# Differential mixer: projection halves and early output units are given other blocks to run beside

## The chip, the cores and the metric

The kernel runs on one core of a Trainium2 chip. Its metric is the device time of one execution in microseconds (us). The engines are TensorE (PE, with its weight loads as PEld), VectorE (DVE), ScalarE (ACT), GpSimd (POOL) and SyncE (SP), which issues the transfers. Each runs its own instructions in the order of the program and waits for the others on semaphores.

## The reference

One layer of an encoder, 1024 tokens of width 1024, all in float32. What matters here is the mixer:

```python
xn = rms_norm(h, norm_mix[i])
proj = xn @ w_in[i]
qa, ka, va, qb, kb, vb = jnp.split(proj, SPLITS, axis=-1)
oa = sliding_window_sink_attention(qa, ka, va, sinks[i], bias_a)     # 8 heads, window 128
ob = differential_attention(qb, kb, vb, lam, ...)                    # 4 heads, 8 blocks of 128 queries
h = h + jnp.concatenate([oa, ob], axis=-1) @ w_out[i]

# differential_attention, for the 128 queries from qs, with all keys below qe = qs + 128:
sc = einsum('bqhmd,bkhmd->bhmqk', q[:, qs:qe], k[:, :qe]) * (HEAD_DIM ** -0.5)   # m = 0, 1
sc = where(allowed, sc + bias, NEG_INF)
pr = softmax(sc, axis=-1)
a = pr[:, :, 0] - lam * pr[:, :, 1]
outs.append(einsum('bhqk,bkhe->bqhe', a, v[:, :qe]))
```

A gated feed-forward part, a gate on a second input and a last norm follow.

## The kernel before

Every float32 product is made as three products of high and low parts (`SPLIT3`), so each operand is split by a copy on ScalarE (high part) and a subtraction on VectorE (low part).

**The differential mixer** is a loop over 32 blocks and a few more steps to drain it: block n is head n // 8 and query block n % 8, with n % 8 + 1 key tiles of 128. It is a pipeline over three iterations. In iteration n, PE runs `b_score(n)` (scores of both maps, into PSUM banks 1 to 4), then a filler, then the turning of earlier results (`y_turn`, the transposes on L1832), the transposes of block n - 1 (L1849) and the product of block n - 2 with V. Block n's scores wait until the exponentials of block n - 1 are done (`b_exp`), since there is one set of score banks. VectorE runs `b_diffs(n - 1)`, which starts with a RECIPROCAL (L1287), then the low part of the transposed block n - 2 (`a_t`), low parts of turned results, `b_logits(n)` (L1304 minima, L1306 bias and minimum, for both maps), then what belongs to fillers. ScalarE copies high parts and then runs `b_exps(n)` (L878). GpSimd normalises the results.

**Fillers.** Two kinds of work that belong to other stages are laid into this loop on PE:

- *Projection halves.* A unit is one 128-column tile of w_in times 512 tokens: 24 matmuls into bank 0, cut into two halves of 12. `b_fill(n)` says which half iteration n carries: 20 halves, two to a unit, in blocks 0 to 19. The last half of a unit is followed by its copy on ScalarE behind the block's exponentials (`unit_hi`) and its low part on VectorE (`unit_lo`, L1181 or L1179) ahead of the next reciprocal.
- *Early output units.* An output unit `c_unit(c)` is 6 matmuls, rows 0 and 1 of w_out times 128 tokens; VectorE adds its sum to `h` (`c_add`, L1319). There are 16: `c_units(n)` puts one in each of blocks 22 to 31 and two in each of iterations 32, 33 and 34. All up to unit 10 use bank 0, later ones banks 0 and 1 in turn (`c_bank`), and a unit waits until its bank's last sum is added. Unit 0 also waits for the reload of `mix_a` (transfers `mix_a_back`, `act_t<-mix_a`), and SP issues that once all projection units are done (`unit_done`, L508), as it overwrites their operand.

`WO_SPLITS` says in which iteration a row block of w_out is split; rows 0 and 1 wait for `unit_done` too, and unit 0 for them. After the last output unit (`c_done`, L522) SP reloads the second half of `mix_a`, for the rest of the output product. That stage, the feed-forward part and the gate follow.

On VectorE and ScalarE the order inside an iteration is that of the code:

```python
            if 2 <= n < NBS:
                b_logits(n)
            pending_w(n)
            part = b_fill(n)
            if part is not None and part % 2 == 1:
                unit_lo(FIRST_UNITS + part // 2)
            for c in c_units(n):
                c_add(c)
            for x in WO_SPLITS.get(n, ()):
                wo_low(x)
```

Of the kernel before, what the change touches and what calls it, by code (L numbers as in the profile page):

```python
# [23 lines left out]
KD = D // P  # L24
NT = SEQ // P
# [38 lines left out]
def build(nc, x, p, w_in, w_out, sinks, lambda_q, lambda_k, subln_gain, rel_bias, norm_mix, norm_ffn,  # L64
# [17 lines left out]
    first = ExitStack()  # L82
# [193 lines left out]
    S = type("S", (), sems)  # L276
# [20 lines left out]
    NUNIT = 2 * NTILE  # L297
# [3 lines left out]
    NA, NBS = 2 * NT, BH * NT  # L301

    HALVES = 2 * (NUNIT - FIRST_UNITS)

    def a_fill(n):
        return n if n < NA + 2 else None

    def b_fill(n):
        return NA + 2 + n if n < HALVES - NA - 2 else None


    def turned_with(n):
# [8 lines left out]
        return psf[:, at:at + P]  # L321

    C_ROWS = 2
    C_FROM = 22
    VIA_DRAM = 2 * NT

    def c_units(n):
        if n < C_FROM:
            return ()
        if n < NBS:  # L330
            return (n - C_FROM,)
        first = NBS - C_FROM + 2 * (n - NBS)
        return tuple(c for c in (first, first + 1) if c < 2 * NT)

    def c_bank(c):
        return c % 2 if c > NBS - C_FROM else 0


    O_ROWS = (4, 5, 6, 2, 3, 7)
    WO_ORDER = (0, 1) + O_ROWS  # L340

    WO_SPLITS = {20: (0,), 21: (1,), 25: (2,), 26: (3,), NBS + 1: (4,), NBS + 2: (5,), NBS + 3: (6,), NBS + 4: (7,)}

    def mix_dst(m, part):
        hh, i = m // NT, m % NT
# [451 lines left out]
    def _(act):  # L797
# [130 lines left out]
        for n in range(NBS + 5):  # L928
            if 2 <= n <= NBS + 1:
                act.wait_ge(S.b_turned, n - 1)  # L930
            for m in turned_with(n - 1):
                act.wait_ge(S.b_yturned, turned_with(n - 1)[-1] + 1)
                if 2 <= m < VIA_DRAM:
                    act.wait_ge(b_stored[m % 2], 16 * (m // 2))
                if m == VIA_DRAM:
                    act.wait_ge(S.unit_done, NUNIT)
                copy(mix_dst(m, 0), y_bank(n - 1, m), S.b_yhi)
            if 2 <= n <= NBS + 1:
                m = n - 2
                w = P * (m % NT + 1)  # L940
                act.wait_ge(S.b_turned, m + 1)
                if m >= 1:
                    act.wait_ge(S.b_pv, m)
                if m == 4:
                    act.wait_ge(S.a_stored, 16 * NA)
                copy(a_t[:, 0, 0:w], psf[:, 5 * HALF:5 * HALF + w], S.b_thi)
            if 3 <= n <= NBS + 2:
                m = n - 3
                act.wait_ge(S.b_pv, m + 1)
                if m >= 1:  # L950
                    act.wait_ge(S.b_sq, m)
                act.wait_ge(S.b_diff, m + 1)
                col = 4 * (m % 4)
                nc.scalar.activation(o_sb[:, :, :], ps[:, 7, 0:2 * P].rearrange("p (a q) -> p a q", a=2), ACT.Copy,  # L954
                                     scale=small[:, col:col + 1]).then_inc(S.b_part, 1)
            pending_w(n)
            for x in WO_SPLITS.get(n, ()):
                wo_hi(x)
            if 2 <= n < NBS:
                b_exps(n)  # L960
            part = b_fill(n)
            if part is not None and part % 2 == 1:
                unit_hi(FIRST_UNITS + part // 2)
            if 3 <= n <= NBS + 2:
                m = n - 3
                act.wait_ge(S.b_sum, m + 1)
                square(o_t[:, :], sq_out, stat[:, 16 + 3 * (m % 2):17 + 3 * (m % 2)], S.b_sq)
# [708 lines left out]
    def _(pe):  # L1676
# [38 lines left out]
        def unit(u, part=None):  # L1715
            j, half = u // 2, u % 2
            if part != 1:
                pe.wait_ge(S.w_lo, j + 1)
                if u == 0:
                    pe.wait_ge(S.xlo0, NT)  # L1720
                if u < FIRST_UNITS:
                    if u >= 2:
                        pe.wait_ge(S.unit_lo, u - 1)
                else:
                    pe.wait_ge(S.unit_lo, u)
            for k in range(KD) if part is None else range(KD // 2 * part, KD // 2 * (part + 1)):
                for n, (a, b) in enumerate(SPLIT3):
                    ins = mm(ps[:, unit_bank(u), :], w_sl[:, j % 2, a, k, :],
                             act_t[:, b, k, HALF * half:HALF * (half + 1)],
                             k == 0 and n == 0, k == KD - 1 and n == 2)  # L1730
            if part != 0:
                ins.then_inc(S.unit_done, 1)

        def c_unit(c):
            t, half = c // 2, c % 2
            if c == 0:
                pe.wait_ge(S.wo_lo, C_ROWS)
                pe.wait_ge(S.mix_c, 16 * 4 * C_ROWS)
                pe.wait_ge(S.unit_lo, NUNIT)
            elif c == NBS - C_FROM + 1:  # L1740
                pe.wait_ge(S.b_exp, 2 * NBS)
            else:
                pe.wait_ge(S.c_added, c - 1 if c_bank(c - 1) != c_bank(c) else c)
            for k in range(C_ROWS):
                for n, (a, b) in enumerate(SPLIT3):
                    ins = mm(ps[:, c_bank(c), :], act_t[:, a, k, t * P:(t + 1) * P],
                             wo(k, b)[:, HALF * half:HALF * (half + 1)], k == 0 and n == 0, k == C_ROWS - 1 and n == 2)
            ins.then_inc(S.c_done, 1)
# [85 lines left out]
        for n in range(NBS + 2):  # L1834
            if 2 <= n < NBS:
                b_score(n)
            if b_fill(n) is not None:
                unit(FIRST_UNITS + b_fill(n) // 2, b_fill(n) % 2)
            for c in c_units(n):
                c_unit(c)  # L1840
            if 2 <= n <= NBS + 1:
                pe.wait_ge(S.b_tlo, n - 1)
            y_turn(n)
            if 1 <= n <= NBS:
                m = n - 1
                nk = m % NT + 1
                pe.wait_ge(S.b_diff, m + 1)
                for k in range(nk):
                    ins = nc.tensor.transpose(psf[:, 5 * HALF + k * P:5 * HALF + (k + 1) * P],  # L1849
                                              e_t[:, m % 2, 0, k * P:(k + 1) * P], ident[:, :])  # L1850
                ins.then_inc(S.b_turned, 1)
            if 2 <= n <= NBS + 1:
                m = n - 2
                hb, nk = m // NT, m % NT + 1
                if m == 0:
                    pe.wait_ge(S.a_olo, NA)
                pe.wait_ge(S.b_tlo, m + 1)
                if m >= 1:
                    pe.wait_ge(S.b_part, m)
                for k in range(nk):  # L1860
                    mm(ps[:, 7, 0:2 * P], a_t[:, 0, k * P:(k + 1) * P], v_b[:, k, hb, :], k == 0, False)
                    ins = mm(ps[:, 7, 0:P], a_t[:, 1, k * P:(k + 1) * P], v_b[:, k, hb, 0:P], False, k == nk - 1)
                ins.then_inc(S.b_pv, 1)

        def oproj(i, rows):
            t = O_TILE[i]
# [260 lines left out]
```

## Time and profile before

| | us |
|---|---|
| median of 3 runs (1274.5 to 1275.2) | 1275.17 |
| the profiled execution | 1275.12 |
| its span, first to last instruction | 1273.3 |
| PE busy | 1213.6 (95%) |
| PEld busy | 993.5 (78%) |
| DVE busy | 875.3 (69%) |
| ACT busy | 519.1 (41%) |
| POOL busy | 321.3 (25%) |
| granted TensorE clock, mean | 0.994 |

Busy is the time in which an engine had an instruction in work. The 32 blocks of the differential mixer run from about 205 to 407 us of the span. A row of the trace in order of time tells the start, the length, the engine, the line, the operation, what it writes and reads and in what shape, how many like it stand together, and in brackets how long the engine was idle before and who ended that wait. Line numbers are those of the kernel before. Matmul rows of different shapes at one line are merged where they follow each other, so the shape is that of the first.

### The profile page before, as it was taken

How to read it: one execution, taken by the hardware profiler on the slowest of the kernel's cores; microseconds unless marked ns; L12 is line 12 of the kernel's file. 1: busy time of each engine (PE TensorE's matmuls, PEld its weight loads, DVE VectorE, ACT ScalarE, POOL GpSimd, SP SyncE). 2: the span in 40 equal slices, each digit the busy share in tenths (PEclk: the TensorE clock that was granted, in tenths of full speed). 3: DMA queues.
4: the chain of work that ended last, by engine and by line, in shares of the span. 5: the costliest groups of instructions: out<-in, count | busy, mean ns of one | idle time of the engine just before them, and what ended most of it. 6: DMA issues, size and time to landing. Idle time of an engine off the chain costs nothing.

```text
span 1273.3 us, 16978 instructions
## 1 busy us (share of the span) xinstructions
PE 1213.6 (95%) x6103; PEld 993.5 (78%) x6103; DVE 875.3 (69%) x1466; ACT 519.1 (41%) x1042; POOL 321.3 (25%) x335
## 2 busy tenths in 40 slices
PE   4999999999789899999999999999999999999997
PEld 3997787788567777888888888888887768888885
DVE  3432786876787477877787777877769997864442
ACT  3322665565564224433333333333344434633321
POOL 0000000354455122232322323313217870000000
PEclk9999999999899999999999999999999999999999
DMA  7364132112831511333322333323497534520101
GB/s 205 73 98 95 42 92 68 46 42 71 210 130 40 159 50 55 104 110 97 121 87 83 124 100 108 98 85 108 149 357 250 166 102 137 186 75 25 42 34 50
DMA packets 128669, 136.08 MB, mean 107 GB/s; under 512 B 15570, under 2 KB 93130, under 8 KB 128522
## 3 DMA queue, kind: packets, MB, share of 16 engines
q1 hardware_dynamic: 128586, 135.00, 35.3%
q8 instruction: 49, 0.80, 0.3%
q14 instruction: 34, 0.28, 0.1%
HBM read 96.77 MB, written 37.22 MB: 105 GB/s over the span
## 4 chain that ended last, share of the span: by engine, by line
PE 56%; DVE 8%; issue 3%; DMA 1%; ACT 0%; SPq 0%; POOL 0%; POOLq 0%; DVEq 0%; ACTq 0%
PE ps L1678 54%; DVE wbuf L1179 4%; DVE more L1179 1%; DVE h L1604 1%; DMA raw<-u_ops 1%; PE ps L1688 1%; DMA act_t<-mix_a 1%; DVE xs L1463 0%; PE ps L1899 0%; DVE h L1458 0%; DVE conv L1402 0%; SPq L479 0%; POOL stat L678 0%; ACT xs L802 0%; DVE act_t L1179 0%
## 5 line engine op out<-in xcount | busy, mean ns | idle before, releaser
L1678 PE MATMUL ps<-act_t,wbuf 128*128 128x512 f32 x1200 | 288.8, 396 | 2.9 <-DVE wbuf L1179 2.9
L1678 PEld LDWEIGHTS ps<-act_t,wbuf 128*128 128x128 f32 x1200 | 225.7, 188 | 57.4 <-issue 3.3
L1678 PE MATMUL ps<-wbuf 128*128 128x512 f32 x912 | 217.5, 392 | 2.6 <-DVE wbuf L1179 2.5
L1678 PEld LDWEIGHTS ps<-wbuf 128*128 128x128 f32 x912 | 170.0, 188 | 42.0 <-DVE wbuf L1179 5.3
L1678 PE MATMUL ps<-act_t,wq 128*128 128x512 f32 x624 | 155.7, 402 | 3.6 <-DVE wq L1181 2.8
L1678 PEld LDWEIGHTS ps<-act_t,wq 128*128 128x128 f32 x624 | 114.6, 189 | 33.5 <-issue 7.3
L1179 DVE TENSOR_TENSOR wbuf<-raw,wbuf 128x512 fp32r<-128x512 f32 (+1 forms) x107 | 104.8, 980 | 13.4 <-ACT wbuf L799 13.1
L678 POOL TENSOR_TENSOR stat<-stat 128x1 f32<-128x1 f32 x32 | 17.6, 549 | 347.6 <-DVE stat L1188 347.6
L799 ACT ACTIVATE wbuf<-raw 128x512 fp32r<-128x512 f32 (+1 forms) x107 | 69.2, 648 | 88.2 <-PE ps L1678 70.4
L1678 PE MATMUL ps<-hx,wbuf 128*128 128x512 f32 x408 | 96.2, 391 | 0.0
L1678 PEld LDWEIGHTS ps<-hx,wbuf 128*128 128x128 f32 x408 | 76.5, 188 | 16.6
L1678 PE MATMUL ps<-wbuf,act_t 128*128 128x512 f32 x288 | 72.7, 407 | 3.2 <-DMA act_t<-mix_a 3.2
L878 ACT ACTIVATE e_t<-ps,small 128x128 f32<-128x128 f32 (+7 forms) x64 | 47.3, 740 | 62.3 <-DVE small L1306 61.2
L799 ACT ACTIVATE wbuf<-xs 128x512 fp32r<-128x512 f32 x66 | 39.8, 624 | 76.6 <-DVE xs L1402 54.2
L1678 PEld LDWEIGHTS ps<-wbuf,act_t 128*128 128x128 f32 x288 | 54.0, 192 | 16.1 <-issue 3.6
L1678 PE MATMUL ps<-wq,act_t 128*128 128x384 f32 (+1 forms) x384 | 59.5, 315 | 0.3 <-DVE act_t L1179 0.3
L1678 PEld LDWEIGHTS ps<-wq,act_t 128*128 128x128 f32 x384 | 57.8, 193 | 0.7 <-DVE act_t L1179 0.7
L1678 PE MATMUL ps<-act_t,more 128*128 128x512 f32 x240 | 58.2, 395 | 0.0
L694 POOL TENSOR_TENSOR o_t<-o_sb 128x128 f32<-128x128 f32 x32 | 14.7, 458 | 170.8 <-ACT o_sb L954 166.8
L705 POOL TENSOR_TENSOR wbuf_f<-wbuf_f 128x512 f32<-128x512 f32 x33 | 52.0, 1576 | 19.0 <-DVE wbuf_f L1542 16.0
L1179 DVE TENSOR_TENSOR a_t<-ps,a_t 128x512 fp32r<-128x512 f32 (+4 forms) x64 | 44.6, 715 | 17.7 <-ACT a_t L799 17.5
L1678 PEld LDWEIGHTS ps<-act_t,more 128*128 128x128 f32 x240 | 45.2, 188 | 10.6
(197 smaller groups left out, 2043.9 us busy)
## 6 DMA issues: line engine op xcount, KB each, us to landing
u_ops<-wbuf_f SPq DMA_DIRECT2D x77, 256.0 KB, 2.2
raw<-u_ops SPq DMA_DIRECT2D x77, 256.0 KB, 2.7
raw<-in_w_ffn_in SPq DMA_DIRECT2D x33, 512.0 KB, 3.9
g_ffn<-in_w_ffn_in SPq DMA_DIRECT2D x11, 512.0 KB, 4.1
act_f<-in_w_ffn_out SPq DMA_DIRECT2D x21, 256.0 KB, 3.9
w_raw<-in_w_in SPq DMA_DIRECT2D x10, 512.0 KB, 4.5
wbuf_f<-in_w_ffn_out SPq DMA_DIRECT2D x18, 256.0 KB, 6.6
x_in<-in_x SPq DMA_DIRECT2D x8, 512.0 KB, 3.6
```

The lines of the kernel that those rows point to most:

```text
L678: nc.gpsimd.tensor_tensor(dst, src, stat[:, 63:64], ALU.pow).then_inc(done, 1)
L694: nc.gpsimd.tensor_tensor(o, o_sb[:, 0, :], o_sb[:, 1, :], ALU.add).then_inc(S.b_sum, 1)
L705: nc.gpsimd.tensor_tensor(dst, a, b, ALU.subtract).then_inc(done, 1)
L799: nc.scalar.activation(dst, src, ACT.Copy, scale=scale).then_inc(done, 1)
L878: nc.scalar.activation(e_t[:, pr, m, 0:w], psf[:, at:at + w], ACT.Exp, scale=-1.0, bias=small[:, o + 2 + m:o + 3 + m], accum_out=small[:, ...
L1179: ins = nc.vector.tensor_tensor(dst, src, hi.bitcast(F32), ALU.subtract)
L1604: nc.vector.tensor_tensor(h[:, t, HALF_X[n]], ps[:, banks(r)[i % 4], :], h[:, t, HALF_X[n]], ALU.add).then_inc(S.h_fin, 1)
L1678: return nc.tensor.matmul(dst, lhs, rhs, start=start, stop=stop)
L1688: ins = nc.tensor.transpose(psf[:, bank * HALF + k * P:bank * HALF + (k + 1) * P], src[:, k * P:(k + 1) * P], ident[:, :])
```

## The change

The 20 projection halves go to blocks 0 to 6, 8 to 14 and 16 to 21: blocks 7 and 15, which have 8 key tiles, lose theirs, and 20 and 21 get one. The 16 output units start in block 25 instead of 22: one in block 25, two in each of 26, 27 and 28, one in 29, none in 30 and 31, then two, three and three. In iterations with more than one, PE runs the first where it stood, ahead of the transposes, and the others behind the product with V; VectorE's order stays as it is. All up to unit 8 use bank 0. The splits of w_out rows move by one or two blocks. The last unit takes its operand's tiles 4 to 7 first, and ScalarE's first write into that operand waits for that half alone (`vproj`) instead of for all units.

```diff
+    B_FILL = dict(zip((0, 1, 2, 3, 4, 5, 6, 8, 9, 10, 11, 12, 13, 14, 16, 17, 18, 19, 20, 21), range(NA + 2, HALVES)))
+
     def b_fill(n):
-        return NA + 2 + n if n < HALVES - NA - 2 else None
+        return B_FILL.get(n)
...
-    C_FROM = 22
...
+    C_FIRST = {25: 0, 26: 1, 27: 3, 28: 5, 29: 7, 30: 8, NBS: 8, NBS + 1: 10, NBS + 2: 13, NBS + 3: 16}
+
     def c_units(n):
-        if n < C_FROM:
-            return ()
-        if n < NBS:
-            return (n - C_FROM,)
-        first = NBS - C_FROM + 2 * (n - NBS)
-        return tuple(c for c in (first, first + 1) if c < 2 * NT)
+        return tuple(range(C_FIRST[n], C_FIRST[n + 1])) if n in C_FIRST and n + 1 in C_FIRST else ()

     def c_bank(c):
-        return c % 2 if c > NBS - C_FROM else 0
+        return c % 2 if c > C_FIRST[NBS] else 0
...
-    WO_SPLITS = {20: (0,), 21: (1,), 25: (2,), 26: (3,), NBS + 1: (4,), NBS + 2: (5,), NBS + 3: (6,), NBS + 4: (7,)}
+    WO_SPLITS = {22: (0,), 23: (1,), 26: (2,), 27: (3,), NBS + 1: (4,), NBS + 2: (5,), NBS + 3: (6,), NBS + 4: (7,)}
...
                 if m == VIA_DRAM:
-                    act.wait_ge(S.unit_done, NUNIT)
+                    act.wait_ge(S.vproj, NT + 1)
...
-            for k in range(KD) if part is None else range(KD // 2 * part, KD // 2 * (part + 1)):
+
+            order_k = (4, 5, 6, 7, 0, 1, 2, 3) if u == NUNIT - 1 else range(KD)
+            ks = order_k if part is None else order_k[KD // 2 * part:KD // 2 * (part + 1)]
+            for k in ks:
...
             if part != 0:
                 ins.then_inc(S.unit_done, 1)
+            elif u == NUNIT - 1:
+                ins.then_inc(S.vproj, 1)
...
-            elif c == NBS - C_FROM + 1:
+            elif c == C_FIRST[NBS] + 1:
                 pe.wait_ge(S.b_exp, 2 * NBS)
...
-            for c in c_units(n):
+            for c in c_units(n)[:1]:
                 c_unit(c)
...
                 ins.then_inc(S.b_pv, 1)
+            for c in c_units(n)[1:]:
+                c_unit(c)
```

## Rows read from the trace of the kernel before

**Rows 1.** In order of time, PE alone: scores of blocks 12 and 20 and those after.

```profile
276.96 1.25 PE L1678 MATMUL ps<-wq 64*128 64x512 f32 x12
...
282.33 1.31 PE L1678 MATMUL ps<-wq 64*128 64x512 f32 x12
...
323.29 1.25 PE L1678 MATMUL ps<-wq 64*128 64x512 f32 x12
...
328.67 1.31 PE L1678 MATMUL ps<-wq 64*128 64x512 f32 x12 [1.15 <-ACT e_t L878]
```

**Rows 2.** The same view, blocks 22 to 24: scores, units 0 and 1, transposes of 23.

```profile
334.22 1.49 PE L1678 MATMUL ps<-wq 64*128 64x512 f32 x12 [0.66 <-ACT e_t L878]
339.23 2.90 PE L1678 MATMUL ps<-act_t 128*128 128x512 f32 x6 [3.52 <-issue]
...
346.49 1.65 PE L1678 MATMUL ps<-act_t 128*128 128x512 f32 x6
...
354.23 1.06 PE L1849 MATMUL ps<-ident,e_t 128*128 128x128 f32 x8 [0.79 <-DVE a_t L1179]
```

**Rows 3.** In order of time, SP's queue: the two reloads of `mix_a`.

```profile
326.04 6.64 SPq L479 DMA_DIRECT2D act_t<-mix_a  x8
...
407.04 5.58 SPq L479 DMA_DIRECT2D act_t<-mix_a  x8
```

**Rows 4.** In order of time, VectorE: the reciprocals of blocks 21 to 23, 29 to 31.

```profile
334.19 0.17 DVE L1287 RECIPROCAL small<-small 128x2 f32<-128x2 f32 x1
...
342.84 0.15 DVE L1287 RECIPROCAL small<-small 128x2 f32<-128x2 f32 x1
...
351.19 0.17 DVE L1287 RECIPROCAL small<-small 128x2 f32<-128x2 f32 x1 [0.72 <-ACT e_t L878]
...
380.86 0.17 DVE L1287 RECIPROCAL small<-small 128x2 f32<-128x2 f32 x1 [0.52 <-ACT e_t L878]
...
387.01 0.17 DVE L1287 RECIPROCAL small<-small 128x2 f32<-128x2 f32 x1 [0.62 <-ACT e_t L878]
...
393.80 0.17 DVE L1287 RECIPROCAL small<-small 128x2 f32<-128x2 f32 x1 [0.73 <-ACT e_t L878]
```

**Rows 5.** In order of time, ScalarE and VectorE: the end of block 15.

```profile
300.65 1.12 ACT L878 ACTIVATE e_t<-ps,small 128x1024 f32<-128x1024 f32 x1
...
302.38 0.69 DVE L1181 SCALAR_TENSOR_TENSOR wq<-ps,wq 128x512 fp32r<-128x512 f32 x1 [1.76 <-ACT wq L799]
302.99 0.15 DVE L1287 RECIPROCAL small<-small 128x2 f32<-128x2 f32 x1
```

**Rows 6.** By stage: stretch, PE, PEld, DVE, ACT, POOL busy (count), PEclk, DMA share, GB/s.

```profile
324.50:335.70 11.20, 5.93 (x51) 4.87 (x49) 10.92 (x26) 8.21 (x20) 5.84 (x10) 1.00 0.88 173
335.70:337.20 1.50, 0.01 (x2) 0.00 (x0) 1.50 (x3) 0.00 (x0) 1.32 (x3) 1.00 1.29 244
337.30:343.90 6.60, 4.67 (x16) 4.02 (x17) 3.41 (x10) 2.73 (x7) 2.31 (x6) 0.50 1.11 316
```

**Rows 7.** In order of time, PE: product with V in iteration 31, transposes, units 14 and 15.

```profile
391.27 1.57 PE L1678 MATMUL ps<-v_b,a_t 128*128 128x256 f32 x12
...
396.84 1.06 PE L1849 MATMUL ps<-ident,e_t 128*128 128x128 f32 x8 [0.68 <-DVE a_t L1179]
...
404.07 2.94 PE L1678 MATMUL ps<-act_t 128*128 128x512 f32 x12
```

**Rows 8.** In order of time, VectorE and PE: w_out low part, end of block 28.

```profile
365.13 1.22 DVE L1179 TENSOR_TENSOR wbuf<-raw,wbuf 128x1024 fp32r<-128x1024 f32 x1
...
373.85 0.49 DVE L1306 CUSTOM_DVE_ANT_0 ps<-ps,bias_b,small 128x256 f32<-128x256 f32 x1
...
374.01 0.89 PE L1678 MATMUL ps<-v_b,a_t 128*128 128x256 f32 x6
...
374.28 0.69 DVE L1319 TENSOR_TENSOR h<-ps,h 128x512 f32<-128x512 f32 x1
...
375.35 0.17 DVE L1287 RECIPROCAL small<-small 128x2 f32<-128x2 f32 x1 [0.38 <-ACT e_t L878]
```

More of the change, by code:

```diff
@@ L1729, in unit @@
                              act_t[:, b, k, HALF * half:HALF * (half + 1)],
-                             k == 0 and n == 0, k == KD - 1 and n == 2)
+                             k == order_k[0] and n == 0, k == order_k[-1] and n == 2)
             if part != 0:
                 ins.then_inc(S.unit_done, 1)
+            elif u == NUNIT - 1:
+                ins.then_inc(S.vproj, 1)
         def c_unit(c):
```

## Prediction, made before the changed kernel was run

> **What bounds the kernel now.** I first read the row of 40 slices on the page: TensorE is nearly always busy, so I looked for the stretch that the change touches, the 32 blocks of the differential mixer, block n having n mod 8 + 1 key tiles. Everything outside it is taken as unchanged. There the list of PE's waits and the order of its work in time tell two regimes apart. Where a block with few or middling keys carries a projection half, PE has no idle time: no row of block 12 shows any [rows 1]. From block 20 on it waits ahead of most scores. Its longest wait, 3.52 us and put down to "issue", is that of early output unit 0 in block 22: PE ends the scores at 335.7 and starts the unit at 339.23 [rows 2]. What it waits for is the reload of `mix_a`, whose eight transfers SP issues over 326.04 to 332.7 [rows 3], because it waits for the last projection half, at the end of block 19.
>
> In blocks with many keys VectorE sets the pace, not PE. A block's clock is best read at its RECIPROCAL (L1287): the vector engine then runs, in order, the difference, two low parts, two maxima and two bias additions without a gap and waits only for the second exponential. From one reciprocal to the next it is 6.15 us with 7 key tiles (380.86 to 387.01) and 6.79 with 8 (387.01 to 393.80); blocks 22 and 23 instead took 8.65 and 8.35 (334.19, 342.84, 351.19) [rows 4].
>
> **Part 1: halves taken out of blocks 7 and 15.** A unit's last half also costs VectorE: in block 15 the exponentials end at 301.77 (300.65 + 1.12), but the vector engine first waits for ScalarE's copy of the unit and makes the low part (302.38, 0.69), so the reciprocal starts at 302.99, 1.1 us later than the 0.12 after the exponentials of an undelayed block [rows 5]. Taking the half away gives 1.1 us back at each of blocks 7 and 15. But the units that end at odd blocks 9 to 15 now end at even ones 8 to 14, and their copies delay those: in block 14 VectorE loses 1.1 it did not lose before. Walking the blocks with these durations, with PE-bound ones (unchanged) between, 0.7 us of the first gain is used up by block 13, and 0.5 us is left from block 16 on. Blocks 16 to 19 have the same halves as before, so block 19 ends 0.5 us earlier.
>
> **Part 2: halves in blocks 20 and 21.** Block 12, with a half, takes PE from score to score 276.96 to 282.33, 5.37 us; block 20, without one, 323.29 to 328.67, 5.38 [rows 1]. The half fills time in which PE waited, so it costs nothing. The second half's low part delays the reciprocal of block 21 by 1.1: 334.19 - 0.5 + 1.1 = 334.8. The splits of w_out rows 0 and 1 go two blocks later with it, into the exponentials' time of blocks 22 and 23, and cost about 0.
>
> **Part 3: the stall at unit 0.** SP now sees the last unit done 6.5 us later, at about 332.5, so the reload is issued until 339.1 and lands, with the same 6.5 us behind the last issue as before (332.7 to 339.2), at about 345.6. Queued behind it on SP are the residual rows, the reload of `mix_b` and the w_out rows; they move with it, and their users (block 26 on, and the output product) have over 10 us to spare. Unit 0 stands in block 25, where PE arrives at about 354: the wait is gone. Blocks 22 and 23 run at the undisturbed pace: 334.8 + 6.15 = 340.95, + 6.79 = 347.7, against 351.19. **Shift here: -3.5 us.** The new wait of ScalarE (`vproj` instead of `unit_done`, block 21) is over before it gets there, since the first half of the last unit runs in block 20.
>
> **Part 4: blocks 22 to 24 now hold nothing but their own work.** The granted clock was 1.00 over 324.5 to 335.7, with PE at work 5.93 of 11.2 us, and still in the first 1.5 us of the wait for unit 0; from 337.3 to 343.9 it was 0.50, 1.2 GHz [rows 6]. At the low clock six matmuls took 2.90 us for 1.65 [rows 2]. After the change PE is emptier still around block 24: block 23's product with V ends at about 346.8 (340.95 + 5.83, as 391.27 + 1.57 stands behind 387.01 [rows 4, 7]), six small score matmuls run at 347.8 for 0.55, and the next transposes wait for VectorE until 350.7 (347.7 + 3.04, as 354.23 behind 351.19 [rows 2, 4]). I take one fall of the clock there, felt by 2.6 us of transposes and products that the path goes through. Halving it over part of them costs between 1.1 and 1.7; I take 1.4. The bounds are 0 and the 3.3 that half of 337.3 to 343.9 would be. **Shift after block 25: -2.1.**
>
> **Part 5: pairs of output units in blocks 26, 27 and 28.** PE runs the second unit of a block behind the product with V, and it must wait until the first one's sum is added, as both use bank 0. On VectorE `c_add` of both stands behind the block's bias additions and ahead of the next reciprocal. So the vector engine adds the first sum, waits while PE makes the second, adds that, and only then goes on. In block 28 the first add starts at 374.28; the second unit could start at 374.97 (PE has just finished the product with V, 374.01 + 0.89), takes 1.65, its add starts at 376.75 and the reciprocal at 377.35 instead of 375.35: 2.0 us [rows 8, 2]. In block 27 it is the same chain, 2.0, plus the low part of a w_out row that now stands there, 1.22 [rows 8], together 3.2. In block 26 there was such a row before: 2.5. Taken off: that row leaves block 25, worth 0.4. Sum 2.0 + 3.2 + 2.5 - 0.4 = **7.3 us**, all on VectorE's chain, with the next blocks' score, exponential and transposes behind it. The bounds: 0, if the second unit were done before the bias additions end, and 3 x (0.69 + 1.65 + 0.69) + 1.2 = 10.3 if none of it lay under the exponentials; I take 7.3, as it is worked out from the rows of these same blocks.
>
> What this buys is nothing: in blocks 30 and 31 a unit lay in PE's idle time and its add under the exponential, so 6.15 and 6.79 were reached with it [rows 4]. **Shift at the end of block 31: -2.1 + 7.3 = +5.2.**
>
> **Part 6: the end.** Before, six units stood behind block 31; now eight. In the old frame: unit 8 lies in the gap ahead of the transposes at 396.84, 9 and 10 take the place of 12 and 13, five follow the product with V instead of two: 3 x 1.47 = 4.4 us (404.07 + 2.94 for two) [rows 7]. The add of unit 9 stands ahead of block 31's low part and delays the two y transposes by 1.0, and unit 15 waits 0.3 for its bank. +5.7. SP issues the reload of the second half of `mix_a` only after the last unit, at 407.04 [rows 3], and what follows is of fixed length. So the whole shift stays.
>
> Sum: -3.5 + 1.4 + 7.3 + 5.7 = **+10.9 us**. The profiled execution took 1275.12 (span 1273.3, 1.8 around it), as good as the median of 1275.17; 1275.12 + 10.9 = **1286.0 us**, 0.85% slower.
>
> **Rivals.**
> (a) *The clock falls only once PE does no work at all.* Speaking for it: of the two falls each came in a wait of over 3 us. Against: it had fallen 1.6 us into the wait that began at 335.7 [rows 6]. Part 4 is then 0: 1284.6. The Trainium skill, "TensorE: Matmul & The Clock Gate", section "HAM oscillation — how this bites in real kernels", has this rule, a clock that falls after an idle stretch. By it too the emptied block 24, with its six small matmuls, would keep the clock. The trace of before agrees only loosely, by the instant of the fall just given.
> (b) *The clock falls more often.* PE also gets waits of some 2 us in blocks 15 and 28 and behind block 31, near or above the longest at which it held before block 22. Each fall costs up to 1.7 where PE sets the pace, as behind block 31, and less elsewhere: 1287.5 to 1291.
> (c) *Not slower.* One mechanism, in blocks 26 to 28: the second unit is ready by the time VectorE asks for it, so that a pair costs nothing. It decides at the point where the product with V ends 2.4 us (a unit and an add) before the bias additions do. The whole 7.3 goes, 1278.7, and with no fall of the clock 1277.3, within 0.2% of before. Against it: in block 28 the product ended at 374.90 and the additions at 374.34 [rows 8], and bank 0 has to be emptied in between.
> (d) *The change doesn't do what it says*: unit 0 meets its reload still under way. By Part 3 there are 8 us between, though SP's transfers share the DMA engines with the residual rows. A late one costs what it is late, 1287 to 1290.
>
> **How the numbers follow.** The forecast 0.53, (a) 0.12, (b) 0.16, (c) 0.12, (d) 0.02, and 0.05 for a gain that I don't see. (c) lies half within 0.2% and half above it. That gives faster by over 0.2% 0.05, within it 0.06, slower 0.89; 0.2% (2.5 us) is about what a measurement of this kernel can tell from no change. The range reaches from the upper end of (c), 1278.5, to most of (b), 1290, with the upper bounds of Part 4 (1287.9) and Part 5 (1289.0) inside; it leaves out some 0.15.
>
> **What would show it.** The reciprocal of block 23 at about 347.7, and no PE wait on "issue" there; a granted clock of 0.5 near 350; a VectorE wait of about 1.7 on PE ahead of an `h` addition (L1319) in each of blocks 26, 27 and 28, and their reciprocals 2 us and more behind the exponentials; block 31's about 5 us later than 393.80; the second reload issued near 418. It is wrong above all if those VectorE waits are missing, or if the tail behind block 31 isn't longer by more than the two units.

## The result, and the profile after

The changed kernel takes 1295.84 us (median of 4 runs, 1294.18 to 1296.66) against 1274.94 for the kernel before (4 runs, 1274.5 to 1275.2): ratio 1.0160, 95% interval 1.0145 to 1.0174. It is slower, as forecast, but by 20.9 us and not by 10.9, and outside the range. The profiled execution took 1295.2 with a span of 1293.4, so 20.1 us above the span of before. Later runs of the changed kernel without any alteration gave 1290.27 (1288.46 to 1296.99, 4 runs), 14.4 above the kernel before beside them (ratio 1.0127). So it is not a narrow number, and I come back to that (e6); the forecast is too low by either.

The page of the changed kernel, its row of TensorE's busy time and of its granted clock in 40 slices of 32 us:

```profile
span 1293.4 us, 16978 instructions
...
PE   4999999899787899999999999999999999999997
...
PEclk9999999998888899899999999999999999999999
```

The five 8s, slices ten to fourteen, are 291 to 453 us: the second half of the differential mixer and the stretch behind it. By stage, the mixer, first in the changed kernel, then in the one before (columns as in [rows 6]):

```profile
203.00:425.00 222.00, 194.00 (x1158) 158.42 (x1157) 155.03 (x383) 117.10 (x322) 88.03 (x160) 0.92 0.27 79
```

```profile
203.00:407.00 204.00, 182.68 (x1159) 148.78 (x1158) 153.44 (x382) 117.32 (x322) 87.62 (x158) 0.98 0.30 86
```

VectorE and ScalarE are busy nearly as long as before; PE does the same matmuls and needs 11.3 us longer, at a mean clock of 0.92 instead of 0.98. So far more matmuls ran slowed than I had reckoned with. What of it lay on the path, busy time doesn't say.

VectorE's reciprocals of blocks 21 to 23 and 29 to 31 in the changed kernel, in order of time, for [rows 4]:

```profile
336.58 0.15 DVE L1285 RECIPROCAL small<-small 128x2 f32<-128x2 f32 x1
...
342.82 0.17 DVE L1285 RECIPROCAL small<-small 128x2 f32<-128x2 f32 x1 [0.18 <-ACT e_t L876]
...
350.01 0.17 DVE L1285 RECIPROCAL small<-small 128x2 f32<-128x2 f32 x1 [0.19 <-ACT e_t L876]
...
391.48 0.17 DVE L1285 RECIPROCAL small<-small 128x2 f32<-128x2 f32 x1 [0.51 <-ACT e_t L876]
...
397.63 0.17 DVE L1285 RECIPROCAL small<-small 128x2 f32<-128x2 f32 x1 [1.17 <-ACT e_t L876]
...
404.54 0.17 DVE L1285 RECIPROCAL small<-small 128x2 f32<-128x2 f32 x1 [1.27 <-ACT e_t L876]
```

The two kernels stand 0.15 us apart already at block 6, ahead of the change; all shifts below are taken from there. Block 21 is 2.2 us later than before (expected +0.6), block 23 1.3 earlier (expected 3.5), block 31 10.6 later (expected 5.2). The last output unit's addition comes 18.0 us later (expected 10.9), the stretch behind it, with the second reload and the matmuls that follow, is 1.2 longer, and the rest of the kernel 0.8.

The change has its own wait of VectorE. VectorE's work in block 27 of the changed kernel, in order of time:

```profile
372.62 0.49 DVE L1304 CUSTOM_DVE_ANT_0 ps<-ps,bias_b,small 128x256 f32<-128x256 f32 x1
...
373.03 0.69 DVE L1317 TENSOR_TENSOR h<-ps,h 128x512 f32<-128x512 f32 x1
375.54 0.69 DVE L1317 TENSOR_TENSOR h<-ps,h 128x512 f32<-128x512 f32 x1 [1.82 <-PE ps L1676]
376.15 1.40 DVE L1177 TENSOR_TENSOR wbuf<-raw,wbuf 128x1024 fp32r<-128x1024 f32 x1
377.47 0.15 DVE L1285 RECIPROCAL small<-small 128x2 f32<-128x2 f32 x1
```

This is the chain that Part 5 worked out: first sum, 1.82 us of waiting for PE's second unit, second sum, low part of a w_out row, and only then the reciprocal.

And the clock. Stretches of the changed kernel in which it was granted 0.50, 1.2 GHz, all of them before 600 us:

```profile
299.50:306.20 6.70, 5.83 (x23) 4.97 (x23) 4.77 (x13) 4.72 (x13) 3.25 (x5) 0.50 0.68 245
340.50:347.10 6.60, 5.18 (x24) 3.93 (x23) 5.96 (x11) 4.55 (x10) 3.12 (x5) 0.50 1.17 265
354.10:360.80 6.70, 6.70 (x29) 5.67 (x28) 2.74 (x8) 2.67 (x10) 2.29 (x5) 0.50 1.06 389
381.40:388.10 6.70, 6.12 (x21) 4.39 (x22) 3.19 (x8) 2.19 (x7) 2.28 (x5) 0.50 0.01 4
395.10:398.30 3.20, 3.20 (x18) 3.08 (x16) 1.93 (x8) 2.65 (x7) 0.36 (x3) 0.50 0.00 0
408.70:412.00 3.30, 3.30 (x16) 3.20 (x15) 0.00 (x0) 0.74 (x3) 1.82 (x4) 0.50 0.00 0
436.00:442.70 6.70, 5.53 (x13) 4.39 (x14) 1.24 (x2) 1.06 (x1) 0.00 (x0) 0.50 0.51 178
518.00:524.60 6.60, 5.88 (x15) 4.64 (x16) 3.07 (x5) 0.63 (x1) 0.00 (x0) 0.50 0.02 5
```

Six falls lie in the mixer, where before had one (the wait for unit 0) and I had forecast one. The seventh stands at the end of the wait for the second reload; before had one there too, at 419, but 3.4 us long. The eighth has no counterpart in before.

### The profile page after: what moved, and what is told of

Same layout as the page of the kernel before. It is cut to its first block, busy times and chain, and to the rows that moved or that the text cites. A ratio compares the mean times of both kernels' runs of the same rounds, so it can differ in the third digit from the quotient of the medians.

```text
span 1293.4 us, 16978 instructions
## 1 busy us (share of the span) xinstructions
PE 1227.9 (95%) x6103; PEld 1006.2 (78%) x6103; DVE 877.5 (68%) x1466; ACT 518.2 (40%) x1042; POOL 319.8 (25%) x335
## 4 chain that ended last, share of the span: by engine, by line
PE 53%; DVE 9%; issue 3%; DMA 1%; SPq 1%; ACT 0%; POOL 0%; POOLq 0%; DVEq 0%; ACTq 0%
PE ps L1676 52%; DVE wbuf L1177 5%; DVE more L1177 1%; DVE h L1602 1%; PE ps L1686 1%; DMA raw<-u_ops 1%; DMA act_t<-mix_a 1%; DVE xs L1461 0%; PE ps L1904 0%; DVE h L1456 0%; DVE conv L1400 0%; SPq L477 0%; POOL stat L676 0%; DVE act_t L1177 0%; ACT xs L800 0%
## 5 line engine op out<-in xcount | busy, mean ns | idle before, releaser
L1177 DVE TENSOR_TENSOR wbuf<-raw,wbuf 128x512 fp32r<-128x512 f32 (+1 forms) x107 | 106.5, 997 | 12.4 <-ACT wbuf L797 12.1
L1676 PEld LDWEIGHTS ps<-act_t,more 128*128 128x128 f32 x240 | 45.2, 188 | 10.6
```

The costliest lines, as they stand in the source:

```text
L1177: ins = nc.vector.tensor_tensor(dst, src, hi.bitcast(F32), ALU.subtract)
L1676: return nc.tensor.matmul(dst, lhs, rhs, start=start, stop=stop)
```

## The experiments

My theory after the result: Parts 1 to 3, 5 and 6 hold, and what is missing is the clock, which falls wherever the change leaves PE half empty. The rival: a pair of units, or the shifted halves, cost more than worked out, and the clock only shows it. In the table, "block 23" and "block 31" are the shifts of these blocks' reciprocals against before, and "last unit" that of VectorE's addition of output unit 15. The shifts of a kernel are read from one profile of it; its times are of all its runs.

| kernel | median us (range; runs) | ratio, 95% interval | block 23 | block 31 | last unit |
|---|---|---|---|---|---|
| changed | 1295.8 (1294.2–1296.7; 4) | 1.0160 (1.0145–1.0174) | −1.3 | +10.6 | +18.0 |
| e6, the same again | 1290.3 (1288.5–1297.0; 4) | 1.0127 (1.0099–1.0155) | −1.5 | +9.5 | +15.3 |
| e1, waits filled | 1287.7 (1284.9–1289.5; 4) | 1.0095 (1.0072–1.0118) | −3.4 | +5.6 | +11.4 |
| e2, late addition | 1284.9 (1284.2–1285.8; 4) | 1.0076 (1.0056–1.0095) | −1.9 | +4.1 | +9.9 |
| e3, single units | 1281.0 (1278.9–1285.6; 5) | 1.0051 (1.0028–1.0073) | −1.5 | −1.2 | +4.6 |
| e4, old halves | 1290.8 (1287.4–1291.4; 4) | 1.0112 (1.0086–1.0139) | −4.0 | +6.9 | +14.3 |
| e5, old halves, singles | 1281.2 (1279.3–1283.6; 4) | 1.0053 (1.0036–1.0069) | −4.0 | −3.6 | +2.2 |
| e7, before filled | 1275.1 (1272.1–1279.0; 10) | 0.9996 (0.9984–1.0008) | −2.2 | −2.2 | −2.2 |
| e8, from 23, filled | 1274.4 (1272.8–1275.8; 10) | 0.9989 (0.9980–0.9999) | −4.0 | −4.0 | −2.6 |
| e9, e8 without filler in the reload wait | 1275.3 (1270.5–1278.8; 11) | 0.9991 (0.9979–1.0002) | −4.1 | −4.1 | −2.7 |
| e10, from 23 alone | 1275.0 (1271.2–1279.1; 12) | 0.9990 (0.9977–1.0004) | −2.9 | −2.9 | −1.6 |

Beside them, on their chips, the kernel before took 1275.7 (e1 to e4), 1275.9 (e5 to e8) and 1276.3 (e9, e10); the ratios are against that.

**e1_filled: the clock alone.** The changed kernel, with matmuls whose result nobody reads laid into PE's waits. They stand where PE waits anyway, and write a bank that is free there.

```diff
+        WARM = {15: (12, 4), 22: (10, 4), 23: (8, 4), 24: (14, 0), 30: (10, 4), 31: (6, 4), 32: (14, 0)}
...
+            for _ in range(WARM[n][i]):
+                mm(ps[:, 2 if n == NBS else 0, 0:2 * P], v_b[:, 0, 0, 0:P], v_b[:, 1, 0, :], True, True)
```

> The changed kernel with matmuls whose results nobody reads (128 x 256, into a bank that is free at that time) laid into the blocks that the change emptied: 16 in block 15, 14 in 22, 12 in 23, 14 in 24, 14 in 30, 10 in 31, 14 behind unit 8. They fill waits of PE and nothing else is changed. Theory A (the low clock is the missing part: the walk without any fall gives +9.5 us at the last output unit, the trace shows +18.0): the falls near 299, 340, 354, 395 and 408 us go, the one near 381 stays, some 7 us come back, about 1289. Theory B (the missing part lies in VectorE's chain and in waits; the low clock falls mostly on work that was not on the path): no gain, 1295 or more. Up to 3 us of loss under both if the added matmuls delay the transposes.

Measured: 1287.73, 8 us under the changed kernel's first median and 2.5 under its second (e6), near theory A's 1289. By stage, the mixer and the first stretches at which the clock had fallen, and the one at which it still fell:

```profile
203.00:418.00 215.00, 194.18 (x1252) 158.93 (x1251) 154.59 (x382) 116.96 (x322) 88.25 (x160) 0.99 0.28 82
299.50:306.20 6.70, 5.48 (x37) 4.63 (x37) 4.61 (x13) 4.87 (x14) 3.27 (x5) 1.00 0.66 248
340.50:347.10 6.60, 5.57 (x44) 4.80 (x44) 6.28 (x13) 4.69 (x11) 3.12 (x5) 1.00 1.13 300
354.10:360.80 6.70, 6.37 (x42) 5.13 (x41) 5.58 (x19) 4.66 (x15) 3.18 (x7) 1.00 1.02 408
377.50:380.80 3.30, 3.30 (x12) 2.16 (x12) 0.54 (x1) 1.28 (x5) 2.28 (x5) 0.50 0.00 0
```

With 94 matmuls more, the mixer is shorter. The reciprocals of blocks 23 and 31 in this kernel, in order of time:

```profile
347.71 0.17 DVE L1285 RECIPROCAL small<-small 128x2 f32<-128x2 f32 x1 [0.19 <-ACT e_t L876]
...
399.33 0.17 DVE L1285 RECIPROCAL small<-small 128x2 f32<-128x2 f32 x1 [1.27 <-ACT e_t L876]
```

347.71 is the 347.7 of Part 3. 399.33 is 1.7 us above what Parts 1 to 5 give without a fall of the clock (393.80 − 3.5 + 7.3 = 397.6); the fall left at 377.5 is 1.0 of it (below). The clock accounts for 6.7 us at the last unit (18.0 − 11.4, rounded from 18.01 − 11.35) and this 1.0, 7.7 in all. The rival had the whole gap in the pairs or halves, and that is refuted. The 7.7 belongs to the changed kernel's first profile: the second one (e6) stands 3.9 us above e1 at the last unit, so that the clock cost it 4.9 (3.9 and the same 1.0).

**e2_late_add: the pairs' wait.** In blocks 26 to 28 VectorE adds the second unit behind the next block's differences, one iteration later, instead of ahead of its reciprocal.

```diff
             if 2 <= n <= NBS:
                 b_diffs(n - 1)
+            if n - 1 < NBS:
+                for c in c_units(n - 1)[1:]:
+                    c_add(c)
...
-            for c in c_units(n):
+            for c in c_units(n)[:1] if n < NBS else c_units(n):
                 c_add(c)
```

> The changed kernel, but VectorE adds the second sum of blocks 26, 27 and 28 behind the next block's differences instead of ahead of its reciprocal, so it no longer stands still for PE. Theory A (VectorE's wait of 1.8 us for the second unit plus its add stands on the chain, three times; 3.4 in block 28): reciprocals of 26, 27 and 28 come 2.4 us or more earlier after their exponentials, and 5 to 8 us go, 1288 to 1291. Theory B (PE then waits for that add ahead of the next block's first unit and the transposes behind it are as late as before): within 2 us of the changed kernel, 1294 to 1296.

Measured: 1284.94. VectorE in blocks 26 and 27, in order of time:

```profile
366.52 0.69 DVE L1317 TENSOR_TENSOR h<-ps,h 128x512 f32<-128x512 f32 x1
367.12 1.22 DVE L1177 TENSOR_TENSOR wbuf<-raw,wbuf 128x1024 fp32r<-128x1024 f32 x1
368.25 0.16 DVE L1285 RECIPROCAL small<-small 128x2 f32<-128x2 f32 x1
...
369.24 0.68 DVE L1317 TENSOR_TENSOR h<-ps,h 128x512 f32<-128x512 f32 x1
...
373.83 0.16 DVE L1285 RECIPROCAL small<-small 128x2 f32<-128x2 f32 x1
```

The second addition at 369.24 waits for nothing, and from reciprocal to reciprocal it is 5.58 us. In e1 the same two stand at 364.96 and 372.63, 7.67 apart. So the wait was real, and it was the order on VectorE that made it. The additions themselves stay, and block 31 is at +4.1. The total is 10.9 us under the changed kernel's first median, more than theory A's 5 to 8, and 5.3 under its second. Not all of it is the wait: the clock was low at 304.1 and from 351.9 to 362.1 in this profile and nowhere else before 430, so the falls near 340, 381, 395 and 408 are missing too. How much of this the late addition did, and how much is chance (see e6), one profile can't tell.

**e3_singles: no pairs.** The changed kernel with its halves, but one output unit in each of blocks 24 to 31.

```diff
-    C_FIRST = {25: 0, 26: 1, 27: 3, 28: 5, 29: 7, 30: 8, NBS: 8, NBS + 1: 10, ...}
+    C_FIRST = {24: 0, 25: 1, 26: 2, 27: 3, 28: 4, 29: 5, 30: 6, 31: 7, NBS: 8, NBS + 1: 10, ...}
```

> The changed kernel with its 8 early output units one to a block in blocks 24 to 31 instead of in pairs in 26 to 28; the eight behind block 31 as they are. Theory A (pairs cost some 8.4 us on VectorE's chain without the clock, and the emptied blocks 24, 30 and 31 lower the clock): both go, 1281 to 1284. Theory B (pairs are cheap, the tail is what costs): 1292 or more. In either case it stays above the kernel before, for the tail's 5.7 us less the 3.5 of the stall: 1277 or more.

Measured: 1281.03, as theory A had it, and 6.7 under e1 although the clock still falls at 298.2 and 339.1. From block 25 to 31 it becomes 1.1 later against before. The units in blocks 24 and 25, and in 30 and 31, cost nothing, and they keep PE busy: no fall lies between 346 and 424.

**e4_old_halves: the other half of the change.** The halves stay in blocks 0 to 19, the units are placed as in the changed kernel.

```diff
-    B_FILL = dict(zip((0, 1, 2, 3, 4, 5, 6, 8, 9, 10, 11, 12, 13, 14, 16, 17, 18, 19, 20, 21), range(NA + 2, HALVES)))
+    B_FILL = dict(zip(range(20), range(NA + 2, HALVES)))
```

> The changed kernel with the projection halves where they were, in blocks 0 to 19, and the new place of the output units. Theory A (moving the halves gives 0.5 us less than 1.1 at block 21, and costs the fall of the clock near 299, some 2 us; but without them blocks 20 to 24 are all empty and the clock falls there once more): within 2.5 us of the changed kernel, 1293 to 1298. Theory B (the halves beside 1024 keys cost time of their own, as the change's name has it): 3 us or more slower than the changed kernel.

Measured: 1290.76, like e6, so theory B is out; the 1293 of theory A was not reached either, by either kernel. With block 15's half back there is no fall at 299. With no halves in 20 and 21 the falls come at 325.6 and 349.5 instead, and then at 370.0, 390.4, 404.1, 3.4 us each. So one thinned stretch is exchanged for another.

**e5_old_singles: old halves and single units.** Both edits above together; what is left of the change is that the units begin in block 24.

> Both moves undone but the number of units: projection halves in blocks 0 to 19, early output units one to a block in blocks 24 to 31, the eight behind block 31 as in the changed kernel. Against the run with single units and the new halves it shows the halves alone. Theory A (the new halves cost the fall of the clock behind block 15 and the unit's low part at block 21, a few us): 1277 to 1279. Theory B (the halves' move is neutral, as the walk ahead of the prediction had it, -0.5 then +1.1): 1280 to 1282. By the sum of parts: -4.0 for the stall, +5.8 for the longer end, so 1.8 above the kernel before.

Measured: 1281.22, which is theory B's number, the same as e3, whose halves are the changed kernel's. In the profiles theory A has something for it: block 23 is 2.4 us earlier than in e3, and the last unit too. That does not show in the total, of which both have a spread of over 4 us. At the last unit the profile stands at +2.2, near the 1.8 of the sum of parts; the profile has 1.4 more behind it and 0.6 ahead of block 6. Against e4 it is 9.5 less: that is what the pairs, with the falls around them, cost.

**e6_after_again: the changed kernel once more,** no edit.

> The changed kernel once more, unaltered, beside the others of this set, since the kernel before spread from 1272 to 1278 us in the last one. Every theory: 1293 to 1298, 19 to 22 us above the kernel before of the same set.

Measured: 1290.02, 1290.52, 1288.46 and 1296.99; three of the four lie under what every theory had. The profile shows falls at 298.4, 339.4, 353.0, 380.3 and 390.6, of 6.8, 6.8, 3.4, 3.4 and 6.8 us: five and not six in the mixer, two of them half as long. The same instructions meet another number of falls in another execution. Behind block 31, for example, PE waited 2.72 us in the changed kernel and the clock fell at 408.7; in e6 it waited 2.92 and the clock stayed at 1.00. TensorE there in order of time, first in the changed kernel, then in e6:

```profile
407.59 1.06 PE L1852 MATMUL ps<-ident,e_t 128*128 128x128 f32 x8 [2.72 <-DVE act_t L1177]
```

```profile
405.89 1.06 PE L1852 MATMUL ps<-ident,e_t 128*128 128x128 f32 x8 [2.92 <-DVE act_t L1177]
```

Between the two profiles the falls make 2.7 us at the last unit, of 5.2 us in all. That the clock makes the whole 5.6 us between the medians, or the 8.5 between single executions, is not shown: one run of the changed kernel took 1296.66 us at a mean clock of 0.987, one of e6 1290.52 at 0.988.

**e7_before_filled: is the clock worth anything before the change?** The kernel before with unread matmuls in blocks 20 to 22, and 12 more ahead of the wait for the second reload.

```diff
+        WARM = {20: (10, 6), 21: (12, 3), 22: (24, 0)}
...
+                            for _ in range(12):
+                                mm(ps[:, 4, 0:P], ident[:, :], ident[:, :], True, True)
                         pe.wait_ge(S.mix_23, 16 * 8)
```

> The kernel before with matmuls whose results nobody reads laid into PE's waits: 16 in block 20, 15 in 21, 24 in 22 ahead of unit 0, and 12 small ones ahead of the wait for the second reload of mix_a. All waits stay as long as they were. Theory A (a low clock costs what the slowed matmuls lose on the path: 2.5 us behind the stall at unit 0, up to 1.7 behind the second wait): 2 to 4 us faster than the kernel before. Theory B (what the clock costs is hidden behind VectorE): no difference.

Measured: 1275.1, ratio 0.9996, no difference. That is theory B's number, but not its reason. The fall at 337 is gone and block 23 is 2.2 us earlier, where 2.5 was expected, and this lasts until the last unit (−2.2). Then it is given back: in the profile the reload, from the last unit's addition on, took 13.4 us (404.49 to 417.88) instead of 11.7. The clock fell behind it for 3.4 us, as in before, and once more at 499.7, where before it did not:

```profile
417.88 14.29 PE L1678 MATMUL ps<-wbuf,act_t 128*128 128x512 f32 x53 [2.18 <-DMA act_t<-mix_a]
```

```profile
417.70:421.10 3.40, 3.22 (x8) 2.56 (x9) 1.12 (x1) 1.06 (x1) 0.00 (x0) 0.51 0.12 47
499.70:503.10 3.40, 3.40 (x11) 2.62 (x10) 1.29 (x2) 0.47 (x1) 0.00 (x0) 0.50 0.00 0
```

**e8_from23_filled, e9_from23_blocks, e10_from23: the good part alone.** The stall at unit 0 can be removed without pairs and without moving a half: units from block 23 on, one each, and seven behind block 31. e8 adds both kinds of filler, e9 those in blocks 20 to 22 only, e10 none.

```diff
-    C_FROM = 22
+    C_FROM = 23
...
-        return tuple(c for c in (first, first + 1) if c < 2 * NT)
+        if n == NBS + 2:
+            return tuple(range(first, 2 * NT))
+        return tuple(c for c in (first, first + 1) if c < 2 * NT) if n < NBS + 2 else ()
...
-        return c % 2 if c > NBS - C_FROM else 0
+        return (c - NBS + C_FROM) % 2 if c > NBS - C_FROM else 0
```

> The kernel before with the early output units one block later, 23 to 31 (nine, and seven behind them), halves as they were, and unread matmuls in the waits of blocks 20 to 22 and ahead of the second reload. Unit 0 should then meet a reload that has landed. Theory A (the stall's 4.0 us go, one more unit at the end costs 1.5, the clock does not fall, 2 to 4): 1269 to 1272. Theory B (the end grows by more than the one unit, as the adds stand ahead of the last low part): 1273 or more.

> Output units from block 23 on and unread matmuls in blocks 20 to 22, as in the last set's fastest, but nothing laid into the wait for the second reload of mix_a. There, both kernels with matmuls in that wait had a reload of 13.4 and 13.6 us, against 11.7 to 11.9 in the others. Theory A (the matmuls in the wait slow the transfers down): the reload takes 11.7 to 11.9 again, the clock falls behind the wait, and the two cancel: 1273 to 1275. Theory B (the longer reload has another cause): 13 us or more here too, 1275 to 1277.

> The kernel before with its early output units in blocks 23 to 31 and seven behind them, and nothing else changed or added. Theory A (the stall of block 22 goes, -4.0; one more unit behind block 31 +1.4; the clock falls once near 337 while blocks 20 to 22 are empty, +1 or less as it meets work hidden behind VectorE): 1273 to 1275.5. Theory B (the fall of the clock takes back what the stall gave): 1275.5 or more.

Measured: 1274.42, 1275.30 and 1274.95, ratios 0.9989, 0.9991 and 0.9990. Only e8's interval ends under 1, at 0.9999; these are a tenth of a per cent, if anything, and no clear winner. e8 came out as theory B had it, e9 between its two theories, e10 as theory A. The table says why: the stall gives 4.0 us with the filler (2.9 without, as the clock still falls at 337.0), the seventh unit behind block 31 takes 1.4 of it, and the fall of the clock at 497 to 499 or the longer reload takes more. The reload took 13.6 us in e8, 12.4 in e9 and 12.0 in e10. That the fillers in the wait lengthen it is the likely reading of e7 and e8, but it rests on one profile each, and the cause stays open.

## Why the prediction was wrong, step by step

**Part 1** (+1.1 back at blocks 7 and 15, 0.5 left) held: blocks 7 and 15 each gain 1.1, block 16 stands 0.9 earlier in both profiles of the changed kernel, where the walk had 0.5, and block 17 0.5 earlier in e1. That last figure is of a kernel with unread matmuls in block 15; no run has the new halves there with neither them nor a fall. **But it missed what block 15 became.** With no half and eight key tiles PE is nearly empty there, and the clock fell at 299.5. TensorE in that place in the changed kernel, in order of time:

```profile
294.46 1.66 PE L1676 MATMUL ps<-wq 64*128 64x512 f32 x12
298.18 0.30 PE L1835 MATMUL ps<-ident,bias_a 128*128 128x128 f32 x1 [2.06 <-DVE mst L1177]
298.32 0.93 PE L1852 MATMUL ps<-ident,e_t 128*128 128x128 f32 x7
299.00 2.44 PE L1676 MATMUL ps<-v_b,a_t 128*128 128x256 f32 x12
302.31 0.90 PE L1676 MATMUL ps<-wq 64*128 64x128 f32 x6 [0.87 <-ACT e_t L876]
303.14 4.24 PE L1676 MATMUL ps<-act_t,wq 128*128 128x512 f32 x11
```

Score matmuls that take 0.55 took 0.90, and behind them stands a half. Block 17 is 1.2 us late, 1.7 later than in e1.

**Part 2** (halves in 20 and 21 free, low part 1.1) held: in e1 block 17 is at −0.5 and block 21 at +0.5.

**Part 3** (no stall, block 23 at 347.7) held with the clock kept, 347.71 in e1. In the changed kernel there is no PE wait on "issue" either, and from block 21 to 23 it takes 6.24 and 7.19 us where I had 6.15 and 6.79. The 0.4 in the second is the fall at 340.5. TensorE there, in order of time:

```profile
339.20 0.30 PE L1835 MATMUL ps<-ident,bias_a 128*128 128x128 f32 x1 [1.95 <-POOL bias_a L701]
339.34 0.82 PE L1852 MATMUL ps<-ident,e_t 128*128 128x128 f32 x6
339.91 1.98 PE L1676 MATMUL ps<-v_b,a_t 128*128 128x256 f32 x10
342.84 2.93 PE L1676 MATMUL ps<-wq 64*128 64x512 f32 x12 [0.95 <-ACT e_t L876]
...
353.06 1.06 PE L1852 MATMUL ps<-ident,e_t 128*128 128x128 f32 x8 [2.38 <-DVE act_t L1177]
```

These are block 23's scores. They took 2.93 us, where the same twelve matmuls took 1.66 at the full clock in e1 (from 340.94), and still only 0.4 shows: VectorE has its differences and low parts to do meanwhile, and waits 0.31 for them.

**Part 4 is the step that failed,** by its count more than by its price. It took one fall, near 350, for 1.4 us, with 3.3 as its upper bound. There were six, for 7.6 us. What each cost is how much more the shift of the changed kernel grows over the blocks where it lies than that of e1, which has no fall there. For block 28, where e1 has a fall too, the measure is e4, which has none there.

| fall at | seen between blocks | changed grows by | without a fall | cost, us | e6 grows by |
|---|---|---|---|---|---|
| 299.5 | 16 and 17 | +2.1 | +0.4 | 1.7 | +1.9 |
| 340.5 | 22 and 23 | −1.2 | −1.6 | 0.4 | −1.2 |
| 354.1 | 23 and 26 | +4.7 | +2.2 | 2.5 | +3.7 |
| 381.4 | 27 and 28 | +3.6 | +2.4 (e4) | 1.3 | +3.5 |
| 395.1 | 28 and 31 | +0.1 | 0.0 | 0.1 | +0.3 |
| 408.7 | 31 and the last unit | +7.4 | +5.8 | 1.6 | +5.8 |

Together 7.6. That is the 7.7 of e1 in its parts and no second measurement of it; what it adds is that the two kernels part only where a fall lies, and run side by side, within 0.1 us, over blocks 17 to 22 and from 26 to 27. The mean of 1.3 is near my 1.4, but the fall that I did forecast cost 2.5, and those at blocks 15 and 28 and behind block 31 were left to rival (b) at a chance of 0.16. They are just its three places, at no more than its price of 1.7 (4.6 in sum). So (b) is the mechanism that happened. Its number, 1287.5 to 1291, lies under the 1295.8 that was measured first and takes in the 1290.3 of later. The walk's premise let me down: a wait of PE was taken to cost nothing wherever VectorE sets the pace, without asking block by block how much work PE has left.

Rival (a), that only a stretch without any work loses the clock, is refuted too. What PE did just ahead of the falls at 299.5, 340.5 and 354.1 in the changed kernel, by stage:

```profile
295.90:299.30 3.40, 1.34 (x13) 1.15 (x11) 3.37 (x5) 0.40 (x2) 2.40 (x4) 1.00 0.10 34
337.10:340.40 3.30, 1.35 (x13) 1.23 (x12) 3.27 (x7) 1.20 (x2) 2.23 (x4) 1.00 1.21 237
350.60:353.90 3.30, 0.92 (x11) 0.88 (x9) 2.87 (x7) 1.57 (x5) 2.94 (x4) 1.00 1.20 290
```

It was at work in each, and its longest waits were 2.06, 1.95 and 2.38 us. The Trainium skill, "TensorE: Matmul & The Clock Gate", section "HAM oscillation — how this bites in real kernels", puts the danger in single idle gaps beyond a length; here the clock was lost over waits with work between them, all shorter than the 3.52 us of [rows 2]. What I said in favour of (a) was read loosely as well: the second fall of before, at 419.1, came just behind its wait of 3.22 us and not in it, as PE had been at work since 418.86. What decides between a fall and none at one place stays open; the wait ahead doesn't do it alone (2.92 us in e6 without a fall).

**Part 5** (2.5 + 3.2 + 2.0 − 0.4 = 7.3) held, a little short. In e1 the shift grows by 9.0 from block 23 to block 28, of which 1.0 is its own fall (block 28 there 3.4, in e4 without a fall 2.4). So 8.0: block 26 3.0, block 27 3.4, block 28 2.4, and 0.8 off in blocks 24 and 25. The chain is the one drawn: in the changed kernel VectorE waits 1.81 and 1.82 us in blocks 26 and 27, where 1.7 was forecast, and 3.44 in block 28, in the low clock (in e4, at the full clock, 2.18). The reciprocals of the three blocks come 3.6 to 3.8 us behind the exponentials. From block 23 to 31 the shift grows by 9.0 in e1, 6.0 in e2 and 0.3 in e3 and e5. The 6.0 of e2 includes its long fall from 351.9. Rival (c) is out, and (d) too: no PE wait on the reload or on "issue" stands at unit 0.

**Part 6** (+5.7) held: from block 31's reciprocal to the last unit's addition it is 19.1 us in e1, e2, e3, e5 and e6, with eight units behind the block, against 13.3 before, +5.8. In the changed kernel it was 20.7, with the clock at 0.50 over 408.7 to 412.0, after a wait of 2.72 for VectorE. The second reload's issue was forecast near 418. SP's queue in the changed kernel, in order of time; in e1 the row starts at 418.35:

```profile
425.19 1.94 SPq L477 DMA_DIRECT2D act_t<-mix_a  x3
```

**"Everything outside it is taken as unchanged"** was the second error, a smaller one. The reload itself took 11.9 us against 11.7, but the matmuls behind it are 1.0 us slower, as the low stretch is 6.7 us and not 3.4. Some 80 us behind it comes the fall at 518, which before has not, and the feed-forward part's first GELU stands 2.8 us later for it. All twelve profiles agree on this stage: it takes as long as before where the clock stays up (e2, e6), 1.3 to 1.6 us more with a fall of 3.4 us (e1, e3, e7, e8), and 2.7 to 2.8 more with one of 6.8 (the changed kernel, e4, e5, e9, e10).

Then 2.0 us are regained, and that is not the clock. Between the first high-part copies of `act_f` and of `act_t` from `act_f` in the feed-forward part (910 to 1090 us of before) it was 1.00 in all twelve profiles, and yet the stretch took 177.5 to 180.8 us: 177.5 in the changed kernel, 179.4 in before. PE's waits there, for the low parts of weights on VectorE, came to 3.1 us in the changed kernel, 4.1 in before and 5.0 in e9, the longest. So the kernels vary by some 3 us in a place that the change doesn't touch. Both kinds of variation fit the 1272 to 1279 us of the kernel before in later runs, though its profile shows one execution only.

From 10.9 to 20.1, then: rival (b)'s three falls 4.6, the fall near 350 1.1 more than taken, the two others 0.5, the pairs 0.7, part 6 0.1, which makes 17.9 for the 18.0 measured; 1.2 in the stretch with the reload, 0.8 behind it, 0.15 ahead of block 6. In e6's profile the falls come to 4.9 instead of 7.6, and the same sum gives 15.2 at the last unit, where 15.3 was measured.

**On the name of the change.** That no half should lie beside 1024 keys is worth nothing here. A last half there costs 1.1 us of low part on VectorE and fills PE; without it PE waits and loses its clock, for 1.7 at block 15. Two units beside few keys instead of one beside many cost 8.0 us, with no fall of the clock counted, and leave blocks 30 and 31 thin. What was good, the later start of the units, is worth 3 to 4 us at block 23 by itself, of which e10 keeps 1.6 at the last unit.

## What to carry to other kernels

Work that fills another engine's waits has a second use, it holds up the clock: before moving it away from where it costs nothing, price the place that it leaves at half of TensorE's rate, and price it once for each place that becomes thin. When a second piece of work is laid beside the same block, look at the in-order engine that must collect its result, and collect it after that engine's next step for the critical chain, not ahead of it (e2: 7.67 to 5.58 us between two reciprocals).

## What the runs showed of the hardware

- The clock fell with no PE wait over 2.4 us ahead of it (299.5, 340.5, 354.1), and stayed at 0.50 though PE was then busy for all of the stretch (6.70 of 6.70 us from 354.1). One fall cost between 0.1 us (395.1) and 2.5 us (354.1). Near 500 us of the span the cost goes with the length of the low stretch: 1.3 to 1.6 us for 3.4, 2.7 to 2.8 for 6.8 (nine profiles).
- The same program meets different falls in different executions: six in one profile, five in another, and after a wait of 2.92 us none where after 2.72 there was one. The executions of the changed kernel spread over 8.5 us; it was tight (1294.2 to 1296.7) in one set of runs and wide in the next. Four runs of each were not enough to settle a difference of 5 us. Part of the spread has nothing to do with the clock: one stretch of the feed-forward part took 177.5 to 180.8 us at a clock of 1.00 throughout.
- Matmuls with an unread result hold the clock at 1.00 through such stretches and make the kernel shorter, where the clock was on the path (e1). They did nothing for the total of the kernel before (e7); in its profile, what was gained at 337 was lost at the reload and near 500.
- The second reload took 13.4 and 13.6 us from the last addition where matmuls filled the wait for it (e7, e8), 11.7 to 12.4 where none did. I had not expected PE's work to bear on it, and whether it does is not settled.
